# A two-block transformer on one core: the second block's context path set into the first block's tail, and the loop unrolled

## What is computed

```python
x = first_block(x, c, ...)                    # 2 layers, then rms_norm
for l in range(2):                            # second_block
    x, ctx = mixer_layer(x, ctx, c_2, c_ctx_2, ..., ctx_out=(l == 0))

# mixer_layer
h  = x   * (1 + scale)   + shift              # modulated latent
hc = ctx * (1 + scale_c) + shift_c            # modulated context
(q, i, ff, fb, ...)    = split(h  @ w_in)     # latent projections
(qc, ic, ffc, fbc, ..) = split(hc @ w_in)     # context projections, same weights
y  = concat(hgrn2, global attention, differential, windowed) * silu(g)
x_new   = layer_norm(alpha * x   + gate   * (y  @ w_out))
ctx_new = layer_norm(alpha * ctx + gate_c * (yc @ w_out))   # only where ctx_out
```

## Time and profile before

| | |
|---|---|
| median of 3 runs | 1622.04 us (1620.84 to 1623.17) |
| the profiled execution | 1621.03 us, span 1619.3 us from first to last instruction |
| TensorE busy | 1473.4 us, 91% of the span, 8182 matmuls |
| DVE, ScalarE, POOL busy | 533.3, 455.3, 146.5 us |
| mean granted TensorE clock | 0.958 of 2.4 GHz |
| DMA queue for data | 190.8 MB, 33.2% of 16 engines |
| weights, unit to landing | 5.0 us, 176 units issued in the sections |

### The profile page before, as it was taken

The page is one execution under the profiler, slowest core; times in us unless marked ns, Lnnn a source line. Parts: engine busy times, 40 slices in busy tenths (PEclk is TensorE's granted clock), DMA queues, the critical chain, the costliest instruction groups (busy, mean ns, idle before and its releaser), DMA issues.

```text
span 1619.3 us, 21024 instructions
## 1 busy us (share of the span) xinstructions
PE 1473.4 (91%) x8182; PEld 1190.1 (73%) x8182; DVE 533.3 (33%) x1237; ACT 455.3 (28%) x771; POOL 146.5 (9%) x193
## 2 busy tenths in 40 slices
PE   5799999999899999999999899879979897888974
PEld 3677888888778788888887677656758685666753
DVE  1163222103153112202222365683242404375221
ACT  1112332300212332300114333434431324233422
POOL 0110200000010210000000041330000001132000
PEclk9999999999999999999999899979989998999977
DMA  9644343555353443454612212212201121110200
GB/s 371 239 178 148 139 156 131 178 186 206 107 186 127 162 146 135 171 185 165 223 58 73 80 51 79 105 53 79 105 26 64 41 104 52 53 53 27 78 0 26
DMA packets 27169, 192.16 MB, mean 119 GB/s; under 512 B 3648, under 2 KB 3776, under 8 KB 4032
## 3 DMA queue, kind: packets, MB, share of 16 engines
q1 hardware_dynamic: 27072, 190.81, 33.2%
HBM read 189.75 MB, written 1.05 MB: 118 GB/s over the span
## 4 chain that ended last, share of the span: by engine, by line
PE 77%; DVE 11%; ACT 6%; issue 3%; DMA 2%; POOL 1%; DVEq 0%; SPq 0%; ACTq 0%; POOLq 0%
PE event L750 38%; PE event L743 9%; PE event L922 7%; PE event L898 5%; PE logits L834 3%; PE mixed_out L886 2%; DMA ring<-in_w 2%; PE turns L853 2%; PE event L706 2%; PE event L1015 1%; ACT S L1125 1%; PE event L914 1%; PE event L768 1%; DVE region L1686 1%; DVE stat L1407 1%
## 5 line engine op out<-in xcount | busy, mean ns | idle before, releaser
L750 PE MATMUL event<-u,ring 128*128 128x256 f32 x3200 | 717.8, 383 | 14.4 <-DMA ring<-in_w 7.6
L750 PEld LDWEIGHTS event<-u,ring 128*128 128x128 f32 x3200 | 608.2, 192 | 118.1 <-issue 31.0
L743 PE MATMUL event<-ring,u 128*128 128x256 f32 (+1 forms) x704 | 154.7, 379 | 0.3 <-DVE region L1644 0.3
L743 PEld LDWEIGHTS event<-ring,u 128*128 128x128 f32 x704 | 131.2, 195 | 24.7 <-issue 7.4
L1732 POOL TENSOR_TENSOR raw<-raw,tables 128x512 f32<-128x512 f32 (+1 forms) x28 | 33.4, 1194 | 1059.3 <-DVE turned L1395 838.1
L922 PE MATMUL event<-region,ring 128*128 128x256 f32 x544 | 119.4, 380 | 0.0
L922 PEld LDWEIGHTS event<-region,ring 128*128 128x128 f32 x544 | 102.9, 190 | 15.2 <-issue 1.5
L1125 ACT ACTIVATE S<-logits,stat 128x512 f32<-128x512 f32 (+2 forms) x160 | 83.9, 535 | 92.2 <-DVE stat L1429 88.0
L834 PE MATMUL logits<-region 64*128 64x256 f32 (+4 forms) x320 | 65.3, 511 | 46.0 <-ACT PT L1141 21.3
L1078 ACT ACTIVATE region<-event 128x512 f32<-128x512 f32 x44 | 26.3, 598 | 241.9 <-PE event L750 241.8
L898 PE MATMUL event<-region,ring 128*128 128x256 f32 x384 | 83.5, 379 | 0.0
(11 more groups left out here) (199 smaller groups left out, 1305.5 us busy)
## 6 DMA issues: line engine op xcount, KB each, us to landing
ring<-in_w SPq DMA_DIRECT2D x176, 1024.0 KB, 5.0
tables<-in_two SPq DMA_DIRECT2D x1, 1600.0 KB, 7.9
x<-in_x SPq DMA_DIRECT2D x1, 1024.0 KB, 16.0
x<-in_ctx SPq DMA_DIRECT2D x1, 1024.0 KB, 11.7
out<-x SPq DMA_DIRECT2D x1, 1024.0 KB, 3.9
tables<-in_one SPq DMA_DIRECT2D x1, 832.0 KB, 12.4
consts<-in_common SPq DMA_DIRECT2D x1, 320.0 KB, 3.0
par<-in_par SPq DMA_DIRECT2D x1, 180.0 KB, 13.4
```

The lines of the kernel that those rows point to most:

```text
L743: ins = mm(bank[:, t * 256:t * 256 + width], mem.u[:, q, k, t * P:(t + 1) * P], wt[:, k * 256:k * 256 + width], start=k == 0, stop=k == KB ...
L750: ins = mm(bank[:, j * 256:(j + 1) * 256], wt[:, k * 256 + j * P:k * 256 + j * P + P], mem.u[:, q, k, :], start=k == 0, stop=k == KB - 1)
```

## The change

The loop over the first block's layers is unrolled into `one0` and `one1`, and `finale` is gone: its items stand at the end of `one1`. All waits are on constants.

- `prologue` keeps 8 of 12 modulation units; the other 4 stand in `one0`, with the second layer's 12. The bias of the modulation is added in each `ada`.
- `one1` gets the whole context path of the second block's first layer up to its gate: 15 projections with q=1, the 8 context jobs behind its own 10, the scan, the state, and in its fill the items of its own merge and output.
- `two0` has the latent path of its layer, the context's outputs, mean and var in slots 4 to 8, and the seven context projections, decay and state of the last layer.
- `two1` has the latent path alone.
- Weights that are used for context and latent are now loaded once for each. The second block's tables are loaded within `one1`; a second form of two window masks within `two0`.
- Buffers of the second block are laid out anew so that the context's lie beside the first block's.

```diff
-def jobs_two(ctx_out):
-    out = []
-    for kind in ("G", "N"):
-        out += [Job(kind, qt, [(b, 0), (b, 1)], 2 * T) for qt in (0, 1) for b in (0, 1)]
-        if ctx_out:
-            out += [Job(kind, qt, HALVES[0], T, 1) for qt in (0, 1)]
-    out += [Job("F", qt, [(h // 2, 2 * (h % 2)), (h // 2, 2 * (h % 2) + 1)], 2 * T)
-            for qt in (0, 1) for h in range(4)]
-    if ctx_out:
-        out += [Job("F", qt, [(b, r) for r in range(4)], T, 1) for qt in (0, 1) for b in (0, 1)]
-    return out
+def jobs_ctx():
+    out = [Job(kind, qt, HALVES[0], T, 1) for kind in ("G", "N") for qt in (0, 1)]
+    return out + [Job("F", qt, [(b, r) for r in range(4)], T, 1) for qt in (0, 1) for b in (0, 1)]
+def jobs_latent(layer):
+    out = [Job(kind, qt, [(b, 0), (b, 1)], 2 * T, 0, layer) for kind in ("G", "N") for qt in (0, 1) for b in (0, 1)]
+    return out + [Job("F", qt, [(h // 2, 2 * (h % 2)), (h // 2, 2 * (h % 2) + 1)], 2 * T, 0, layer)
+                  for qt in (0, 1) for h in range(4)]
...
+def of_one(sec, item):
+    if item[0] == "proj":
+        return item[1] in ONE_PROJ
+    return item[0] in ("merge", "out") and sec.block == 1 and item[-1] != (1,)
+def layer_of(sec, q):
+    return q if sec.name == "two0" else sec.layer
+def proj_layer(sec, name, q):
+    return layer_of(sec, q) if name in CARRIED else 0 if q else sec.layer
...
+def script_one0():
+    s, fill = one_start()
+    fill += [[proj("gate", 0, i)] for i in range(6)] + [[proj("m", 0, i)] for i in range(4)]
     s += weave(len(JOBS_ONE), fill) + [i for f in fill for i in f]
     s += [("gates",), ("sig", 0)]
-    s += [proj("m", i) for i in range(4, 8)] + [("sig", 1), ("merge", 0, 0), ("merge", 0, 1)]
-    s += [proj("m", i) for i in range(8, 12)] + [("sig", 2), ("merge", 1, 0), ("merge", 1, 1)]
+    s += [proj("m", 0, i) for i in range(4, 8)] + [("sig", 1), ("merge", 0, 0), ("merge", 0, 1)]
+    s += [proj("m", 0, i) for i in range(8, 12)] + [("sig", 2), ("merge", 1, 0), ("merge", 1, 1)]
     s += [("merge", 2, 0), ("merge", 2, 1)] + [("out", i, (0,)) for i in range(4)]
-    heavy = [n for n, i in enumerate(s) if i[0] in ("proj", "merge", "out")]
-    return modulate(s, heavy[5::7][:6], 2) + [("stats",)]
-def scan_steps(ctx_out):
-    out = []
-    if ctx_out:
-        out += [([("level", 1, LEVELS[i - 2])] if i > 1 else []) + [("prep", 1, m)] for i, m in enumerate(LEVELS)]
-        out += [[("level", 1, LEVELS[-2]), ("prep", 0, "khat")], [("level", 1, LEVELS[-1])], [("hout", 1)], [("sq", "h1")]]
-        out += [[("khatT",), ("norm", "h1")]]
-    else:
-        out += [[("prep", 0, "khat")], [], [("khatT",)]]
-    out += [[("prep", 0, 0)], [("state",)]]
+    groups = [("w0", 4), ("w0", 5)] + [("w1", g) for g in range(6)]
+    s = modulate(s, heavy(s)[3::5][:8], 2, groups)
+    s.insert(s.index(("ada", 5, "w1")) + 1, ("cond",))
+    return s + [("stats",)]
...
+def ctx_scan():
+    out = [([("level", 1, LEVELS[i - 2])] if i > 1 else []) + [("prep", 1, m)] for i, m in enumerate(LEVELS)]
+    out += [[("level", 1, LEVELS[-2]), ("prep", 1, "khat")], [("level", 1, LEVELS[-1])], [("hout", 1)], [("sq", "h1")]]
+    return out + [[("khatT", 1), ("norm", "h1")], [("state", 1)]]
...
+def latent_scan():
+    out = [[("prep", 0, 0)]]
...
+def script_one1():
+    s, fill = one_start()
+    fill[8].append(("small",))
+    fill += [[proj("kk", 1)], [proj("vv", 1)], [proj("gq", 1), ("sq", "gk1")], [proj("gate", 0, 0), ("norm", "gk1")],
+             [proj("gate", 0, 1), ("sq", "gq1")], [proj("gate", 0, 2), ("norm", "gq1")], [proj("gate", 0, 3)],
+             [proj("gate", 0, 4)], [proj("gate", 0, 5)], [proj("hq", 1)], [proj("ff", 1)], [proj("fb", 1)],
+             [proj("hi", 1), proj("nq", 1)], [("gates",), proj("m", 0, 0), ("decay", 1), proj("m", 0, 1)]]
+    tail = [[proj("m", 0, 2)], [proj("m", 0, 3), ("sig", 0)], [proj("fk", 1)], [proj("fq", 1)], [("merge", 0, 0)], [("merge", 0, 1)],
+            [proj("fv", 1)]]
+    tail += [[proj("m", 0, i)] for i in range(4, 8)] + [[("sig", 1), ("merge", 1, 0)], [("merge", 1, 1)]]
+    tail += [[proj("m", 0, i)] for i in range(8, 12)] + [[("sig", 2), ("merge", 2, 0)], [("merge", 2, 1)]]
+    tail += [[("out", i, (0,))] for i in range(4)]
+    jobs = JOBS_ONE + jobs_ctx()
+    at = len(fill)
+    slots = 2 * len(jobs) - at
+    fill += [[] for _ in range(slots)]
+    for n, items in enumerate(tail):
+        fill[at + n * slots // len(tail)] += items
+    for h, items in enumerate(ctx_scan()):
+        fill[min(at + h, len(fill) - 1)] += items
+    s += weave(len(jobs), fill) + [i for f in fill for i in f]
+    s = modulate(s, heavy(s)[2::4][:6], 2, [("v0", g) for g in range(6)])
+    n = s.index(("ada", 3, "v0")) + 1
+    s[n:n] = [("mod", "v0"), ("feed", 1, "v0")]
+    s += [proj("g", 1, 0), ("stats",), proj("g", 1, 1), ("final",), ("feed", 0, "v0"), ("sq", "f1"), proj("g", 1, 2),
+          ("norm", "f1"), proj("g", 1, 3)]
...
+def script_two0():
+    out = lambda i: ("out", i, (1,))
+    s = [proj("kk"), proj("vv"), ("gate", 1, 0), ("gate", 1, 1), ("rot", "nk", 0), ("sq", "gk0"), proj("gq"), ("norm", "gk0"),
+         out(0), ("sq", "gq0"), ("rot", "gk", 0), proj("ff"), ("norm", "gq0"), proj("fb"), ("rot", "gq", 0), ("decay", 0)]
+    jobs = jobs_latent(0)
     fill = [[] for _ in range(2 * len(jobs))]
-    if ctx_out:
-        for h, item in ((0, first("hq", 1)), (1, again("hq", 0)), (2, first("hi", 1)), (3, again("hi", 0)),
-                        (5, first("nq", 1)), (7, again("nq", 0)), (9, ("rot", "nq", 0)),
-                        (10, first("fk", 1)), (12, again("fk", 0)), (14, first("fq", 1)), (14, ("rot", "fk", 0)),
-                        (16, again("fq", 0)), (18, ("rot", "fq", 0)), (19, first("fv", 1)), (21, again("fv", 0))):
-            fill[h].append(item)
-        at = 3
-    else:
-        for h, item in ((0, first("hq", 0)), (1, first("hi", 1)), (3, again("hi", 0)), (5, first("nq", 0)), (6, ("rot", "nq", 0)),
-                        (7, first("fk", 1)), (9, again("fk", 0)), (11, first("fq", 0)), (11, ("rot", "fk", 0)),
-                        (13, ("rot", "fq", 0)), (13, first("fv", 0)), (14, again("fv", 1))):
-            fill[h].append(item)
-        at = 2
-    for h, items in enumerate(steps):
-        fill[at + h] += items
-    at += len(steps)
-    gates = [(first if q == a else again)("g", q, i) for i in range(4) for q in ((a, b) if ctx_out else (0,))]
-    left = len(fill) - 4 - at
-    for n, item in enumerate(gates):
-        fill[at + n * left // len(gates)].append(item)
-    if ctx_out:
-        for g in range(6):
-            h = 4 + 7 * g
-            fill[h] += [("mva", 2 * g), ("mva", 2 * g + 1)]
-            fill[h + 1].append(("ada", g))
-    fill[-4] += [("gate", 0, 0)] + [("gate", 1, 0)] * ctx_out
-    s = start + weave(len(jobs), fill) + [i for f in fill for i in f]
-    if ctx_out:
-        at = max(s.index(("mix", last_differential(jobs, 0))), s.index(("gate", 0, 0))) + 1
-        s[at + 4:at + 4] = [("gate", 0, 1)]
-        s[at + 3:at + 3] = [("norm", "f0")]
-        s[at:at] = [("sq", "f0")]
-        last = len(jobs) - 1
-        s.insert(s.index(("mix", last)), ("out", 1, (0,)))
-        s.insert(s.index(("mix", last - 1)), ("out", 0, (0,)))
-        s += [("sq", "f1"), ("out", 2, (0,)), ("norm", "f1"), ("gate", 1, 1), ("out", 3, (0,))]
-        s += [("out", 0, (1,)), ("mean", 0), ("out", 1, (1,)), ("out", 2, (1,)), ("var", 0), ("out", 3, (1,))]
-        return s + [("mod", 1), ("feed", 0, "next"), ("mean", 1), ("var", 1), ("feed", 1, "next")]
-    s += [("sq", "f0"), ("norm", "f0"), ("gate", 0, 1)]
+    for h, items in ((0, [proj("hq")]), (1, [proj("hi")]), (2, [proj("nq")]), (3, [("rot", "nq", 0)]), (4, [out(1)]), (5, [out(2)]),
+                     (6, [out(3)]), (7, [("mean", 1)]), (8, [proj("fk"), ("var", 1)]), (9, [proj("fq"), ("rot", "fk", 0)]),
+                     (10, [proj("fv"), ("rot", "fq", 0)]), (11, [("mod", "v1"), ("feed", 1, "v1")]),
+                     (12, [proj("g", 0, 0)]), (14, [proj("ff", 1)]), (15, [proj("fb", 1)]), (17, [proj("kk", 1)]),
+                     (18, [proj("hi", 1), ("sq", "gk1")]), (19, [("norm", "gk1")]), (20, [proj("g", 0, 1)]), (22, [proj("g", 0, 2)]), (24, [proj("g", 0, 3)]),
+                     (26, [proj("vv", 1)]), (28, [("gate", 0, 0)])):
+        fill[h] += items
+    for h, items in enumerate(latent_scan()):
+        fill[3 + h] += items
+    for h, items in ((18, [("decay", 1)]), (19, [("prep", 1, "khat")]), (21, [("khatT", 1)]), (23, [("state", 1)])):
+        fill[h] += items
+    for g, h in enumerate((1, 3, 5, 7, 13, 16)):
+        fill[h] += group("v1", g)
+        fill[h + 1].append(("ada", g, "v1"))
+    s += weave(len(jobs), fill)
+    s += [("sq", "f0"), proj("fk", 1), ("norm", "f0"), ("gate", 0, 1)] + [("out", i, (0,)) for i in range(4)]
+    return s + [proj("fv", 1), ("mean", 0), ("var", 0), ("feed", 0, "v1")]
...
+def script_two1():
```

(67 more changed lines are left out.)

929 lines of the change are left out of this document (462 added, 467 removed).

## The result

The kernel after takes 1633.12 us (median; 1628.45 to 1634.03), the kernel before beside it 1621.35 us: 1.0066 times as long, 95% interval 1.0049 to 1.0083. That is 11.8 us slower, where I forecast 1626 us, 5 us slower; it is the mechanism of my forecast, with a cost 7 us higher. The profiled execution of the kernel after has a span of 1631.9 us, against 1619.3 before.

What follows compares the result with a forecast made beforehand. TensorE's work, which the change doesn't cut, plus waits with slower matmuls behind them, nearly all in the start and second block. Start -8.4, context path +4, second block's first layer -2, last layer +11: +5 us, 1626; range 1601 to 1648.

Steps and rivals of the forecast that it cites:

- The start, -8.4: Prologue: with four of twelve modulation units gone, the first projection starts at 37.4 instead of 50.82; net 8.4 us less.
- The context path, +4: First block's second layer: context work hides other engines' chains; 4 us charged for khatT, norm and state in the last slot.
- Rival B: First block's tail isn't dense, slot chains exceed 12.5 us: +22 us, total 1648; chance 0.20.
- rival C: Late weights or tables hold the ring, so context work is waited for: total 1650; chance 0.04.
- var(1), 10: Second block's first layer, slot 8: context norm chain on ScalarE and DVE costs 10 us of wait and slow clock.
- decay(1), 3: Second block's first layer: the decay ahead of the tenth softmax costs 3 us.
- The seam, 13.3: Between the second block's two layers: bare chain from var(0) through feed to the first projection, 13.3 us.
- The last layer, 299: Second block's last layer: loses seven context projections that filled slots; waits rise from 81 to about 92 us.
- Job 3, priced at 7: Last layer's scan slots: job 3 has only 5.4 us of work left, so 7 us of wait.
- The start, priced at 14: Last layer's start: job 0's softmax with no projection over it, 6.8 us; 14 with the slow clock.
- Rival A: The fill suffices: var(1), job 3 and jobs 9 and 12 cost nothing extra, total 1604; chance 0.33.
- the bare jobs 9 and 12: Last layer: F jobs 9 and 12 have no unit to fill them, 5 us each.

Runs made afterwards that it cites:

- var_short: Kernel after with var(1) of the first layer cut to one multiply and one add in place of eight each: 1625.62 us, ratio 1.0024.
- two_back: Kernel after with context projections fk and fv moved back from the first layer into the last layer's slots 0 and 5: 1611.82 us, ratio 0.9950.
- warm_half: Unread matmuls sized to fit the waits, added to a kernel after with context projections and decay re-placed (1594.18 us): 1581.00 us, ratio 0.9760.
- seam_fv: Kernel after with the last layer's context projection fv moved from ahead of mean(0) to behind var(0): 1623.85 us, ratio 1.0012.
- decay_odd: Kernel after with decay(1) moved from slot 18 to slot 17, behind the ninth job's turning: 1625.31 us, ratio 1.0021.

## Why the prediction was right, and where it was off

- **The start, -8.4.** The seam of the passes moved by 7.05 us, and undoing it costs 5.9. The first projection was to start at 37.4; it is at 38.70 here and between 35.91 and 38.70 in the other kernels that share this prologue, as the last reduction ahead of it moves. Differences of this size between the totals are in part this.
- **The context path, +4.** It cost no more than its work: 146.0 us more for 147 counted. The stretch of dense jobs in the earlier trace rows was the right row; the 4 us for khat, norm and state weren't paid (1.55 us of wait stand there). Rival B is refuted, and rival C with it: none of the pass's waits on TensorE is one for weights.
- **var(1), 10** is too high: in the kernel after its place shows 0.89 and 4.17 us of wait and 2.4 of slow matmuls, 7.5 in all, and 5.1 of them went in var_short. **decay(1), 3** is the term that failed most in the first layer: 8.16 us of wait stand there, and 3.3 of slow matmuls behind it. The decay starts only when the projection hi is done, and softmax, norm and the copy come behind it on the same two engines. How much of the 11.5 us is the decay's own no run shows, since none leaves it out; one slot earlier it costs 3.8 us less. **The seam, 13.3** measured 13.20, read off link by link. In the first layer the terms cancel, which is luck: 378 forecast, 379 measured.
- **The last layer, 299**, measured 308.7, 9.7 us more: this is where the forecast is off. The slow first projection behind the seam (10.13 for 7.07) stood in no term, 3 us. Job 3, priced at 7, cost about 11: 6.61 and 0.77 of wait, and 3.6 of slow matmuls behind them. The start, priced at 14, has waits of 3.88 and 8.59 and 3.6 of slow matmuls, 16. My count of its work at full clock, 207, holds as far as can be told: its busy time of 236.9 less 26 to 29 us of slow matmuls, an estimate from its rows, is 208 to 211.
- **The sum.** Forecast: -8.4 + 4 - 2 + 11. Measured: -7 + 0 on the pass, and +20 on the two layers (688 us for 814 less 146). That is 11 us more than forecast on the two layers; a context path without the charged 4 us hid a third of it, so the total came out nearer than its terms.
- **The reason itself**, that thinned stages don't shrink with their work, is shown by two_back, and more strongly than I had it: work put back there made the layer shorter. Rival A had var(1), job 3 and the bare jobs 9 and 12 at nothing; the rows show 5.1 us or more, 11 us, and 3.46 us of wait ahead of the logits behind each of the two.

The prediction held the clock to be a part of each wait. The Trainium skill (TensorE: Matmul & The Clock Gate, Part 1) has the array at 1.2 GHz after an idle spell and at 2.4 GHz once busy; the rows of warm_half agree: logits of 2.08 us behind 3.45 us of idle time, and of 1.13 where most of that time is filled. But a short wait doesn't always slow the next matmuls: behind the same 3.46 us the logits took 1.13 in the earlier trace rows.

## What to carry to other kernels

When work is moved out of a stage that waits for other engines, price the stage by its waits afterwards, not by its work: look which wait each moved unit stood in, above all at a seam where a chain of norm and feed has nothing beside it. Choose the units that can move by what they don't depend on, and put them into the longest waits; here that was worth 39 us with no work taken away. Then look at the second number of each row: where matmuls behind a short wait are slow, work in the wait, even useless, gives their time back, if it fits into the wait and if no other engine's chain sets the time right behind. And price a single edit between the same matmuls of two traces: here the spans of the profiled executions differed by 7 to 11 us for one edit (seam_fv, decay_odd, var_short), and 2 to 6 of them did not stand at the edit's place.

## What the runs showed of the hardware

Unread matmuls in the waits were worth 13 us of 1594: 43 calls of about 0.45 us each (4.05 us for nine). A wait of 3.45 us was enough for 9.51 us in place of 7.07 in the projection behind. The same code ran at different clocks in different executions: from the start of the second block's first layer to the first of its last three outputs, where the scripts of both are the same, the kernel after needed 323.9 us at a mean clock of 0.92 and seam_fv 319.8 at 0.95.
